# Eight expert jobs as one pipeline, with the rows returned through a DRAM scratch and the expert weights in contiguous blocks

## The chip, the cores and the metric

One core of a Trainium2 chip runs the whole program. The metric is the device time of one launch in microseconds; the kernel before has a median of 1696.33 us in 3 runs (1695.38 to 1701.48). The host's work on the inputs ahead of the launch is not in it.

## The reference

Two layers over 256 tokens of width 1024, all in float32:

```
h = h + swa_sink_attention(rms_norm(h), ...)      # layer 0
h = h + swiglu(rms_norm(h), f_gate, f_up, f_down)
h = h + gated_deltanet(rms_norm(h), ...)          # layer 1
h = h + moe(rms_norm(h))
out = rms_norm(h)

def moe(h):                                       # D_FF = 3584, 8 experts, top 2
    logits = h @ w_router;  top_w = softmax(top_k(logits, 2))
    for e in range(8):
        y = (silu(h @ w_gate[e]) * (h @ w_up[e])) @ w_down[e]
        out += combine[:, e:e+1] * y              # combine is 0 where e isn't chosen
```

Each expert has three matrices of 1024 x 3584, 44 MB in float32. On average 64 of the 256 tokens choose an expert.

## The kernel before

Four stages follow each other: attention, FFN, gated DeltaNet (GDN) and the experts. The change is in the last, which starts at about 633 us.

**Precision.** A float32 product is made of three matmuls in the type f32r (mm3, L282 to 285): high by high, high by low and low by high. So each weight block is split in two. `fetch` (L262) brings 1 MB from DRAM to one of six raw slots, `split_high` (L267, ScalarE) rounds it to w_high, `split_low` (L273, VectorE) takes the rest as w_low. The split pair has three slots. Counting semaphores tie these together: a fetch of block n waits until block n-6 has been split low, a high split of n until TensorE has used block n-3.

**A job.** The tokens of an expert are packed into 128 rows ("slots"). A job is one expert on its 128 slots; if an expert has over 128 tokens there is a second job for it, up to 11 in all. In this run there are 8, one for each expert; jobs 8 to 10 are skipped by a test on a value that the kernel computes (`njobs`). A job goes through 7 chunks of 512 columns of D_FF. A chunk uses six blocks: two of gate (0, 1), two of up (2, 3), two of down. For a chunk TensorE does 24 matmuls of gate into PSUM bank 0, 24 of up into bank 1, four transposes of the activation (`turned`, L1275), and 24 matmuls of down that add up in banks 2 and 3 over the job. The gate of the next chunk is issued ahead of `turned` of this one, so that silu (ScalarE) and the product m_act (VectorE) are behind matmuls. In steady state block numbers of a step are 4, 5 (gate of the next chunk), 6, 7 (its up), 8, 9 (down of this one), 10, 11 (gate of the one after), and ScalarE and VectorE take them in this order, with silu, m_act and m_act_high/low between.

**Between jobs.** The last chunk has no gate of a next one beside it. The kernel instead turns the next job's rows (`turn_in`, L1302, eight transposes of x_slots, which ScalarE and VectorE split to x_high and x_low), does `turned` and down, and then, in the next turn of the loop:

- ScalarE and VectorE copy the job's result from banks 2 and 3 as ys_high and ys_low;
- TensorE does gate of the first chunk, then `back(j)` (L1292): eight matmuls of pickT, a 0/1 matrix that puts the slots back to their tokens, into banks 4 to 7; then two matmuls that turn the next `pick` into bank 1, which VectorE copies to pickT, and only then up, which writes bank 1;
- VectorE adds banks 4 to 7, times the router's weight, to h (`add`, L1812), and makes the next `pick`.

The first `back` has no job before it: its operands are cleared to zero (L1805 to 1807). The last follows the loop, and after it the final norm.

**Rows in.** POOL scatters the normed tokens to a DRAM scratch of 12 x 128 rows by indirect DMAs (`fill_slots`), cleared in the FFN stage (`clear_slots`), and loads 128 rows for each job from 1 on. Job 0 gets its rows by a gather on TensorE (L1254 on).

**Reads of the weights.** SP reads w_gate and w_up as [128 partitions x 4 x 512] with rows of 2 KB and w_down as [128 x 2 x 1024] with rows of 4 KB, out of the matrices as they are given.

Of the kernel before, what the change touches and what calls it, by code (L numbers as in the profile page):

```python
# [12 lines left out]
D = 1024  # L13
T = 256
TT = T // 128
# [58 lines left out]
def hybrid_kernel(nc, x, a_norm, a_w_qkv, a_b_qkv, a_sinks, a_w_o, f_norm, f_w_gate, f_w_up, f_w_down,  # L74
                  b_norm, b_w_in, b_conv_w, b_a_log, b_dt_bias, b_o_norm, b_w_o,
                  m_norm, m_w_router, m_w_gate, m_w_up, m_w_down, final_norm, consts, out,
# [12 lines left out]
    with ExitStack() as ctx:  # L89
# [81 lines left out]
        with ExitStack() as c:  # L171
# [23 lines left out]
            xg = sb("x_slots", [128, D], c=c)  # L195
            late, row_e, row_s = (sb(n, R8, c=c) for n in ("late", "row_e", "row_s"))
# [4 lines left out]
        x_dram = nc.dram_tensor("x_slots_dram", ((JOBS + 1) * 128, D), f32, kind="Internal").ap()  # L201
        NJ = 15
# [91 lines left out]
        def _(sp):  # L294
# [45 lines left out]
            if "moe" in stages:  # L340
                def job(j, e):
                    ffn_stream(base["moe"], j * NC, m_w_gate[0, ds(e, 1)], m_w_up[0, ds(e, 1)], m_w_down[0, ds(e, 1)],
                               lambda i: j * NC + i)
# [17 lines left out]
        def _(pool):  # L361
# [18 lines left out]
            def clear_slots():  # L380
                link(nc.gpsimd.memset(zeros[:], 0.0))
                for j in range(JOBS + 1):
                    pool.dma_start(x_dram[128 * j:128 * j + 128, :], zeros[:]).then_inc(sem("slots_clear"), 16)

            def fill_slots():
# [12 lines left out]
                pool.dma_start(xg[:], x_dram[128:256, :]).then_inc(sem("xg_in"), 16)  # L398
                njobs = pool.value_load(jobs[0:1, NJ:NJ + 1], min_val=E, max_val=JOBS)
                with pool.Fori(1, JOBS) as j:  # L400
                    with pool.If(j < njobs):
                        pool.wait_ge(sem("gather_ps"), j + 1)
                        pool.dma_start(xg[:], x_dram[ds((j + 1) * 128, 128), :]).then_inc(sem("xg_in"), 16)
# [83 lines left out]
        def _(act):  # L487
# [111 lines left out]
            def deltanet(n0):  # L599
                act.wait_ge(sem("slots_clear"), 16 * (JOBS + 1))  # L600
                act.dma_start(o_w[:], bcast(b_o_norm[0])).then_inc(loaded_gdn, 16)
# [154 lines left out]
            def experts(n0):  # L756
# [9 lines left out]
                nc.scalar.activation(w1[:], gap[:], ACT.Exp).then_inc(sem("gap_exp"), 1)  # L766

# [14 lines left out]

                act.wait_ge(sem("jobs_done"), 1)
                njobs = act.value_load(jobs[0:1, NJ:NJ + 1], min_val=E, max_val=JOBS)
                with act.Fori(0, JOBS) as j:
                    with act.If(j < njobs):
                        def silu(n, r):
                            act.wait_ge(w_used, n + r * RAW)
                            nc.scalar.activation(mg[:], PS[:, 0, :], ACT.Silu).then_inc(sem("m_silu_done"), 1)

                        def turned(c):
                            act.wait_ge(sem("m_turn_ps"), j * NC + c + 1)
                            nc.scalar.activation(maH[:], PS[:, 4, :].rearrange("p (f q) -> p f q", f=4), ACT.Copy)\  # L793
                                .then_inc(sem("m_high_done"), 1)

                        r0 = j * NC
                        split_high(act, n0 + 2, r0)
                        split_high(act, n0 + 3, r0)
# [3 lines left out]
                        with act.Fori(0, NC - 1) as i:  # L802
                            r = j * NC + i
                            split_high(act, n0 + 6, r)
                            split_high(act, n0 + 7, r)
                            turned(i)
                            split_high(act, n0 + 8, r)
                            act.wait_ge(sem("m_act_done"), j * NC + i + 1)
                            silu(n0 + 6, r)
                            for n in range(9, 12):  # L810
                                split_high(act, n0 + n, r)
                        turned(NC - 1)
                        turned_in(j + 1)
                        with act.If(j + 1 < njobs):
                            split_high(act, n0 + SUBS_FFN, r0)
                            split_high(act, n0 + SUBS_FFN + 1, r0)
                        act.wait_ge(sem("back_ps"), j + 1)
                        act.wait_ge(w_used, n0 + SUBS_FFN + r0 * RAW)
                        nc.scalar.activation(ysH[:].rearrange("p (b n) -> p b n", b=2), PS[:, 2:4, :], ACT.Copy)\
                            .then_inc(sem("ys_high"), 1)  # L820
# [13 lines left out]
        def _(pe):  # L834
# [402 lines left out]
            def experts(n0):  # L1237
# [73 lines left out]
                with pe.Fori(0, JOBS) as j:  # L1311
                    with pe.If(j < njobs):
                        def gate(n, r):
                            gate_up(n, r, 0).then_inc(w_used, 1)

                        def up(n, r):
                            gate_up(n, r, 1).then_inc(w_used, 1)

                        r0 = j * NC
                        pe.wait_ge(sem("gather_low"), j + 1)  # L1320
                        gate(n0, r0)
                        back(j)
# [585 lines left out]
```

## Time and profile before

| | us |
|---|---|
| median of 3 runs | 1696.33 |
| span of the profiled execution | 1695.6 |
| TensorE busy (matmuls) | 1564.9 |
| VectorE busy | 1245.4 |
| ScalarE busy | 1017.5 |
| POOL busy | 79.7 |

The span runs from the first to the last instruction; the device time of the three runs is this and the little that lies around it, so the two stand 0.7 us apart at the median. The profiled execution moved 446.03 MB in 190790 DMA packets, 430.83 MB of them on SP's queue. Matmuls of 512 columns show as 0.39 us each but start every 0.23 us, as they are pipelined: starts tell more than durations. In the rows PEclk is the granted TensorE clock as a share of 2.4 GHz, and a DMA share over 1 means that packets of several queues or blocks overlapped on an engine. "[0.88 <-PE PS L285]" behind an instruction is the time that its engine stood idle ahead of it and what ended that.

### The profile page before, as it was taken

The page shows a single profiled execution, that of the slowest core. Times are in us where ns is not written, and L with a number is a line of the kernel's source. Part 1 is how long each engine was busy: PE and PEld are TensorE (multiplying, and loading weights), DVE is VectorE, ACT ScalarE, POOL GpSimd, SP SyncE. Part 2 cuts the span into 40 slices and gives each one's busy share as a digit, 9 for nine tenths or more (in the row PEclk, how much of TensorE's full clock was granted, in tenths as well). Part 3 has the DMA queues.
Part 4 walks back from the last instruction along what each step waited for, and adds up shares of the span by engine and source line. Part 5 has one row for each costly group of instructions (what it writes and reads, how often), then busy time and mean ns, then how long its engine had stood idle before and what let it go on. Part 6 is the DMA issues. An engine that isn't in the chain of part 4 may idle for free.

```text
span 1695.6 us, 22769 instructions
## 1 busy us (share of the span) xinstructions
PE 1564.9 (92%) x8311; PEld 1308.0 (77%) x8311; DVE 1245.4 (73%) x1044; ACT 1017.5 (60%) x949; POOL 79.7 (5%) x89
## 2 busy tenths in 40 slices
PE   5888999998987877999999999999999999999996
PEld 4777888878986866887887887887887887887885
DVE  4745555545674446888888888888888888888886
ACT  4444434334853334677677677677777777777774
POOL 0002000000223112000000000000000000000000
PEclk9789999999999796999999999999999999999999
DMA  9317655552430212999999999999999999999992
GB/s 329 98 39 275 220 174 194 176 174 100 133 117 28 75 62 97 347 361 351 344 368 349 336 387 337 345 372 344 341 369 351 336 374 349 341 372 339 361 368 88
DMA packets 190790, 446.03 MB, mean 263 GB/s; under 512 B 9632, under 2 KB 10016, under 8 KB 190752
## 3 DMA queue, kind: packets, MB, share of 16 engines
q1 hardware_dynamic: 184032, 430.83, 71.1%
q0 software_dynamic: 3456, 12.58, 1.9%
q10 hardware_dynamic: 3264, 2.08, 0.4%
q8 instruction: 27, 0.44, 0.1%
q14 instruction: 11, 0.09, 0.0%
HBM read 436.03 MB, written 9.44 MB: 263 GB/s over the span
## 4 chain that ended last, share of the span: by engine, by line
PE 84%; DVE 6%; ACT 5%; issue 3%; ACTq 1%; DVEq 1%; POOL 0%; POOLq 0%
PE PS L283 25%; PE PS L285 25%; PE PS L284 25%; DVE w_low L275 2%; ACT w_high L271 2%; PE PS L1277 1%; PE PS L846 1%; PE PS L920 1%; PE PS L1162 1%; ACT xs L520 1%; ACT L271 1%; PE PS L896 0%; PE PS L1153 0%; PE PS L1209 0%; PE PS L909 0%
## 5 line engine op out<-in xcount | busy, mean ns | idle before, releaser
L275 DVE TENSOR_TENSOR w_low<-w_raw,w_high 128x2048 fp32r<-128x2048 f32 x408 | 934.0, 2296 | 247.6 <-ACT w_high L271 247.4
L271 ACT ACTIVATE w_high<-w_raw 128x2048 fp32r<-128x2048 f32 x408 | 781.2, 1917 | 393.9 <-PE PS L285 393.0
L283 PE MATMUL PS<-w_high,x_high 128*128 128x512 f32 x1264 | 503.5, 398 | 23.7 <-DVE pickT L1838 15.1
L285 PE MATMUL PS<-w_high,x_low 128*128 128x512 f32 x1264 | 495.6, 392 | 0.0
L284 PE MATMUL PS<-w_low,x_high 128*128 128x512 f32 x1264 | 494.9, 392 | 0.0
L283 PEld LDWEIGHTS PS<-w_high,x_high 128*128 128x128 f32 x1264 | 239.5, 189 | 76.8 <-DVE w_low L275 22.4
L285 PEld LDWEIGHTS PS<-w_high,x_low 128*128 128x128 f32 x1264 | 238.8, 189 | 51.5
L284 PEld LDWEIGHTS PS<-w_low,x_high 128*128 128x128 f32 x1264 | 239.4, 189 | 48.4
L283 PE MATMUL PS<-w_high,m_act_high 128*128 128x512 f32 x448 | 177.9, 397 | 11.9 <-DVE m_act_low L1831 11.9
L285 PE MATMUL PS<-w_high,m_act_low 128*128 128x512 f32 x448 | 177.2, 395 | 0.0
L284 PE MATMUL PS<-w_low,m_act_high 128*128 128x512 f32 x448 | 177.1, 395 | 0.0
L283 PEld LDWEIGHTS PS<-w_high,m_act_high 128*128 128x128 f32 x448 | 84.2, 188 | 33.3 <-issue 13.8
L285 PEld LDWEIGHTS PS<-w_high,m_act_low 128*128 128x128 f32 x448 | 84.2, 188 | 20.4
L284 PEld LDWEIGHTS PS<-w_low,m_act_high 128*128 128x128 f32 x448 | 84.2, 188 | 19.7
L793 ACT ACTIVATE m_act_high<-PS 128x512 fp32r<-128x512 f32 x56 | 33.6, 599 | 82.3 <-PE PS L1277 82.3
L283 PE MATMUL PS<-x_high,w_high 128*128 128x256 f32 x192 | 57.0, 297 | 0.0
L284 PE MATMUL PS<-x_low,w_high 128*128 128x256 f32 x192 | 55.9, 291 | 0.0
L285 PE MATMUL PS<-x_high,w_low 128*128 128x256 f32 x192 | 55.7, 290 | 0.0
L846 PE MATMUL PS<-cst,xs 128*128 128x128 f32 x96 | 21.6, 417 | 32.6 <-DVE xs L1384 25.2
L1398 DVE TENSOR_TENSOR h<-PS,h 128x512 f32<-128x512 f32 x36 | 22.5, 684 | 32.9 <-PE PS L285 32.9
L283 PE MATMUL PS<-w_high,f_act_high 128*128 128x512 f32 x112 | 45.5, 406 | 1.0 <-DVE f_act_low L1526 1.0
L846 PEld LDWEIGHTS PS<-cst,xs 128*128 128x128 f32 x96 | 19.4, 223 | 34.5 <-DVE xs L1384 26.8
(271 smaller groups left out, 1364.9 us busy)
## 6 DMA issues: line engine op xcount, KB each, us to landing
w_raw<-in_m_w_gate SPq DMA_DIRECT2D x112, 1024.0 KB, 7.2
w_raw<-in_m_w_up SPq DMA_DIRECT2D x112, 1024.0 KB, 7.1
w_raw<-in_m_w_down SPq DMA_DIRECT2D x112, 1024.0 KB, 6.7
w_raw<-in_b_w_in SPq DMA_DIRECT2D x16, 1024.0 KB, 5.5
w_raw<-in_f_w_gate SPq DMA_DIRECT2D x14, 1024.0 KB, 5.1
w_raw<-in_f_w_up SPq DMA_DIRECT2D x14, 1024.0 KB, 5.1
w_raw<-in_f_w_down SPq DMA_DIRECT2D x14, 1024.0 KB, 4.9
w_raw<-in_a_w_qkv SPq DMA_DIRECT2D x6, 1024.0 KB, 13.9
```

Of the source, the lines that this page charges most:

```text
L271: nc.scalar.activation(WH[:, n % SPLIT, :], W[:, n % RAW, :], ACT.Copy).then_inc(hi_done, 1)
L275: nc.vector.tensor_tensor(WL[:, n % SPLIT, :], W[:, n % RAW, :], WH[:, n % SPLIT, :].bitcast(f32), ALU.subtract).then_inc(lo_done, 1)
L283: nc.tensor.matmul(o, sH, mH, start=first, stop=False)
L284: nc.tensor.matmul(o, sH, mL, start=False, stop=False)
L285: return nc.tensor.matmul(o, sL, mH, start=False, stop=last)
L520: nc.scalar.activation(xs[:, t], h[:, t], ACT.Square, accum_out=ss[:, n, t:t + 1]).then_inc(ss_done, 1)
L793: nc.scalar.activation(maH[:], PS[:, 4, :].rearrange("p (f q) -> p f q", f=4), ACT.Copy)\
L846: last = nc.tensor.transpose(PS[:, 4 + b, 256 * kk + 128 * t:256 * kk + 128 * t + 128], src[:, t, 128 * k:128 * k + 128], ident)
L920: last = nc.tensor.matmul(PS[:, 6 + a % 2, 64 * hh:64 * hh + 64], probT[:, a % 2, hh * (t + 1) + kt, :], qkv[:, kt, 1280 + 64 * g:1280 + 6 ...
L1162: last = nc.tensor.matmul(PS[halves(s), A + s, HALF * hh:HALF * hh + HALF], Zt[halves(s), t, hh, :], X[halves(s), t, hh, :], start=True, s ...
L1277: last = nc.tensor.transpose(PS[:, 4, 128 * f:128 * f + 128], ma[:, 128 * f:128 * f + 128], ident)
L1398: return V.tensor_tensor(h[:, t, cb * CH:(cb + 1) * CH], PS[:, bank, :], h[:, t, cb * CH:(cb + 1) * CH], ALU.add)
```

## The change

The loop over jobs 0 to 7 becomes one pipeline of 56 chunks. Every step is the same on each engine: gate of the next chunk, `turned`, up of the next chunk, down of this one, also where the next chunk belongs to the next job. In the step ahead of a job's last, TensorE turns the next job's rows behind up. In the first step of a job ScalarE copies banks 2 and 3 (the result of the job before) to `ys`, and POOL stores that to a second DRAM scratch, `y_slots`. So `back`, pickT and `add` are left out for jobs 0 to 6. After job 6's store POOL gathers, by four indirect DMAs, for every token the row of each of its two experts, and VectorE adds them to h with the weights w0 and w1 while the last down runs. Job 7 (`LAST`) still returns through pickT. Rows 7 x 128 and on of the scratch are cleared to zero in the FFN stage, so that tokens of job 7 and of jobs over 7 add nothing there. Jobs 8 to 10 run, if there are any, one after the other behind that.

The host writes the experts' weights as one array of 1 MB blocks in the order in which they are read, gate, up of a chunk and down of the one before; each block is [128 partitions x 2048] with 8 KB of a partition in one piece. SP reads them one after the other. Block 2 of the first job is now split ahead of the gather instead of behind it.

```
+        y_dram = nc.dram_tensor("y_slots_dram", ((JOBS + 1) * 128, D), f32, kind="Internal").ap()
+        LAST = E - 1
+        Y_CLEAR = JOBS + 1 - LAST
...
+                def fetch_block(n, r, m):
+                    if n >= RAW:
+                        sp.wait_ge(lo_done, n - RAW + 1 + r * RAW)
+                    sp.dma_start(W[:, n % RAW, :], m_w_blocks[m] if isinstance(m, int) else m_w_blocks[ds(m, 1)].rearrange("a p c -> p (a c)"))\
+                        .then_inc(w_in[n % RAW], 16)
+
...
-                with sp.Fori(0, E) as j:
-                    job(j, j)
+                for k in range(4):
+                    fetch_block(n0 + k, 0, k)
+                with sp.Fori(0, E * NC - 1) as q:
+                    for k in range(6):
+                        fetch_block(n0 + 4 + k, q, 6 * q + 6 + k)
+                for k in range(2):
+                    fetch_block(n0 + 4 + k, E * NC - 1, E * SUBS_FFN + 4 + k)
...
+                for j in range(LAST, JOBS + 1):
+                    pool.dma_start(y_dram[128 * j:128 * j + 128, :], zeros[:]).then_inc(sem("y_stored"), 16)
...
+                def store(j):
+                    pool.wait_ge(sem("ys_out"), j + 1)
+                    pool.dma_start(y_dram[ds(j * 128, 128), :], ys[:]).then_inc(sem("y_stored"), 16)
+
+                with pool.Fori(0, LAST - 1) as j:
+                    pool.wait_ge(sem("gather_ps"), j + 2)
+                    pool.dma_start(xg[:], x_dram[ds((j + 2) * 128, 128), :]).then_inc(sem("xg_in"), 16)
+                    store(j)
+                store(LAST - 1)
+                pool.wait_ge(sem("y_stored"), 16 * (Y_CLEAR + LAST))
+                for c in range(2):
+                    for t in range(TT):
+                        nc.gpsimd.indirect_dma_start(yg[:, c, t], None, y_dram[:, :], bass.IndirectOffsetOnAxis(ap=slot[:, c, t:t + 1], axis=0))\
+                            .then_inc(sem("yg_in"), 16)
...
+                split_high(act, n0 + 2)
...
+                def y_out(j):
+                    act.wait_ge(w_used, n0 + 4 + (j + 1) * NC * RAW)
+                    act.wait_ge(sem("y_stored"), 16 * Y_CLEAR + 16 * j)
+                    nc.scalar.activation(ys[:].rearrange("p (b n) -> p b n", b=2), PS[:, 2:4, :], ACT.Copy).then_inc(sem("ys_out"), 1)
+
...
+                def step(q, out_of=None, x_of=None):
+                    split_high(act, n0 + 6, q)
+                    if out_of is not None:
+                        y_out(out_of)
+                    split_high(act, n0 + 7, q)
+                    turned(q)
+                    split_high(act, n0 + 8, q)
+                    act.wait_ge(sem("m_act_done"), q + 1)
+                    silu(n0 + 6, q)
+                    split_high(act, n0 + 9, q)
+                    if x_of is not None:
+                        turned_in(x_of)
+                    split_high(act, n0 + 10, q)
+                    split_high(act, n0 + 11, q)
+
+                split_high(act, n0 + 3)
+                silu(n0 + 2, 0)
+                split_high(act, n0 + 4)
+                split_high(act, n0 + 5)
+                step(0)
+                with act.Fori(0, LAST) as j:
+                    with act.Fori(1, NC - 2) as i:
+                        step(j * NC + i)
+                    step(j * NC + NC - 2, x_of=j + 1)
+                    step(j * NC + NC - 1)
+                    step(j * NC + NC, out_of=j)
+                with act.Fori(LAST * NC + 1, E * NC - 1) as q:
+                    step(q)
+                turned(E * NC - 1)
+                y_high(n0 + 6, E * NC - 1)
...
+                def pick_turned(c):
+                    pe.wait_ge(sem("pick_done"), c + 1)
+                    for t in range(TT):
+                        last = nc.tensor.matmul(PS[:, 7, 128 * t:128 * t + 128], pick[:, t, :], identR[:], start=True, stop=True)
+                    last.then_inc(sem("pickT_ps"), 1)
+
...
+                def step(q, first=False, final=False, x_of=None, x_wait=None, out_of=None):
+                    pe.wait_ge(sem("m_silu_done"), q + 1)
+                    if x_wait is not None:
+                        pe.wait_ge(sem("gather_low"), x_wait + 1)
+                    gate(n0 + 4, q)
+                    pe.wait_ge(sem("m_act_done"), q + 1)
+                    turned()
+                    up(n0 + 6, q)
+                    if x_of is not None:
+                        turn_in(x_of)
+                    pe.wait_ge(sem("m_low_done"), q + 1)
+                    if out_of is not None:
+                        pe.wait_ge(sem("ys_out"), out_of + 1)
+                    down(n0 + 8, q, first, final)
+
                 gather(0)
+                pe.wait_ge(sem("gather_low"), 1)
+                gate(n0, 0)
+                pe.wait_ge(sem("slot_done"), 1)
+                up(n0 + 2, 0)
+                step(0, first=True)
+                with pe.Fori(0, LAST) as j:
+                    with pe.Fori(1, NC - 2) as i:
+                        step(j * NC + i)
+                    step(j * NC + NC - 2, x_of=j + 1)
+                    step(j * NC + NC - 1, final=True, x_wait=j + 1)
+                    step(j * NC + NC, first=True, out_of=j)
+                with pe.Fori(LAST * NC + 1, E * NC - 1) as q:
+                    step(q)
+                pick_turned(1)
+                pe.wait_ge(sem("m_act_done"), E * NC)
+                turned()
+                pe.wait_ge(sem("m_low_done"), E * NC)
+                down(n0 + 4, E * NC - 1, False, True)
+                back(0)
...
+                split_low(dve, n0 + 2)
                 gathered(0)
...
-                V.memset(ysH[:].bitcast(f32), 0.0)
-                V.memset(ysL[:].bitcast(f32), 0.0)
-                V.memset(pickT[:].bitcast(f32), 0.0).then_inc(sem("pickT_done"), 1)
-                dve.wait_ge(sem("pickT_done"), 1)
-                dve.sem_inc(sem("ys_low"), 1)
-                dve.sem_inc(sem("added"), 1)
...
+                def step(q, x_of=None):
+                    split_low(dve, n0 + 6, q)
+                    split_low(dve, n0 + 7, q)
+                    turned(q)
+                    split_low(dve, n0 + 8, q)
+                    split_low(dve, n0 + 9, q)
+                    gated(q + 1, n0 + 8, q)
+                    if x_of is not None:
+                        turned_in(x_of)
+                    split_low(dve, n0 + 10, q)
+                    split_low(dve, n0 + 11, q)
+
+                split_low(dve, n0 + 3)
+                split_low(dve, n0 + 4)
+                gated(0, n0 + 4, 0)
+                split_low(dve, n0 + 5)
+                step(0)
+                with dve.Fori(0, LAST) as j:
+                    with dve.Fori(1, NC - 2) as i:
+                        step(j * NC + i)
+                    step(j * NC + NC - 2, x_of=j + 1)
+                    step(j * NC + NC - 1)
+                    step(j * NC + NC)
+                picks(LAST, slice(0, 128))
+                with dve.Fori(LAST * NC + 1, E * NC - 1) as q:
+                    step(q)
+                turned(E * NC - 1)
+                pick_turned(0)
+                dve.wait_ge(sem("yg_in"), 16 * 2 * TT)
+                for c, weight in enumerate((w0, w1)):
+                    for t in range(TT):
+                        if c:
+                            dve.wait_ge(sem("added"), t + 1)
+                        V.scalar_tensor_tensor(out=h[:, t], in0=yg[:, c, t], scalar=weight[:, t:t + 1], in1=h[:, t],
+                                               op0=ALU.mult, op1=ALU.add).then_inc(sem("added"), 1)
+                dve.sem_inc(sem("added"), 4 * LAST)
+                y_low(0)
+                add(0, LAST)
...
+def expert_blocks(gate, up, down):
+
+    g = gate.reshape(E, 2, 4, 128, NC, CH).transpose(0, 4, 1, 3, 2, 5).reshape(E, NC, 2, 128, SUB)
+    u = up.reshape(E, 2, 4, 128, NC, CH).transpose(0, 4, 1, 3, 2, 5).reshape(E, NC, 2, 128, SUB)
+    d = down.reshape(E, NC, 2, 2, 128, D).transpose(0, 1, 2, 4, 3, 5).reshape(E, NC, 2, 128, SUB)
+    blocks = np.zeros((E * NC + 1, 6, 128, SUB), np.float32)
+    blocks[:E * NC, 0:2] = g.reshape(E * NC, 2, 128, SUB)
+    blocks[:E * NC, 2:4] = u.reshape(E * NC, 2, 128, SUB)
+    blocks[1:, 4:6] = d.reshape(E * NC, 2, 128, SUB)
+    return blocks.reshape(6 * (E * NC + 1), 128, SUB)
```

## Rows read from the trace of the kernel before

**Rows 1.** the page's first part, busy time of each engine

```profile
PE 1564.9 (92%) x8311; PEld 1308.0 (77%) x8311; DVE 1245.4 (73%) x1044; ACT 1017.5 (60%) x949; POOL 79.7 (5%) x89
```

**Rows 2.** stretches: us; PE, PEld, DVE, ACT, POOL busy; PEclk, DMA share, GB/s

```profile
20.00:24.00 4.00, 2.76 (x8) 1.94 (x7) 3.26 (x9) 3.15 (x9) 0.00 (x0) 1.00 1.04 393
801.50:928.00 126.50, 122.86 (x553) 100.35 (x552) 109.98 (x67) 91.52 (x62) 0.54 (x1) 1.00 0.97 354
837.00:854.00 17.00, 17.00 (x77) 13.92 (x77) 14.86 (x8) 12.41 (x9) 0.00 (x0) 1.00 1.03 380
```

**Rows 3.** the chain that ended last, in order of time, of 620 to 830

```profile
691.36 0.44 PE PS L1277 x4
...
776.23 0.44 PE PS L1277 x4
...
787.74 0.87 PE PS L1305 x8
788.62 0.45 PE PS L1277 x4
...
817.50 0.44 PE PS L1277 x4
```

**Rows 4.** TensorE's waits, 676 to 1690: us, times, longest

```profile
PE PS L283 <- DVE pickT L1838: 15.1, 8, 2.5
PE PS L283 <- DVE m_act_low L1831: 11.9, 8, 1.5
PE PS L283 <- DVE w_low L275: 2.8, 8, 0.4
```

**Rows 5.** TensorE in order of time, 663 to 680

```profile
664.97 0.79 PE L283 MATMUL PS<-w_high,x_high 128*128 128x512 f32 x1 [4.55 <-DVE x_low L1769]
...
673.34 0.39 PE L1298 MATMUL PS<-ys_high,pickT 128*128 128x512 f32 x1
...
677.98 0.79 PE L283 MATMUL PS<-w_high,x_high 128*128 128x512 f32 x1 [2.46 <-DVE pickT L1838]
```

**Rows 6.** all engines in order of time, a steady chunk

```profile
1098.36 1.92 ACT L271 ACTIVATE w_high<-w_raw 128x2048 fp32r<-128x2048 f32 x1 [0.88 <-PE PS L285]
...
1102.63 3.12 SPq L265 DMA_DIRECT2D w_raw<-in_m_w_up  x2
...
1109.53 0.40 PE L283 MATMUL PS<-w_high,m_act_high 128*128 128x512 f32 x1
...
1111.80 2.28 DVE L275 TENSOR_TENSOR w_low<-w_raw,w_high 128x2048 fp32r<-128x2048 f32 x1
...
1115.13 0.39 PE L283 MATMUL PS<-w_high,x_high 128*128 128x512 f32 x1
```

**Rows 7.** the blocks w_raw issued from 837 to 854

```profile
DMA to landing us min/median/max: 6.5/7.7/7.8
```

**Rows 8.** x_high and x_low in order of time, end of job 7

```profile
1672.69 1.08 ACT L780 ACTIVATE x_high<-PS 128x512 fp32r<-128x512 f32 x2
...
1673.80 1.29 DVE L1779 TENSOR_TENSOR x_low<-PS,x_high 128x512 fp32r<-128x512 f32 x2 [0.29 <-ACT x_high L780]
```

**Rows 9.** the chain that ended last, 1655 to 1696

```profile
1671.72 0.45 PE PS L1277 x4
...
1679.55 1.03 ACT ys_high L819
...
1680.60 1.24 DVE ys_low L1862
...
1691.27 1.28 DVE fin L1883
```

**Rows 10.** ScalarE in order of time, 655 to 690

```profile
660.46 2.17 ACT L771 ACTIVATE x_high<-PS,cols 128x128 fp32r<-128x128 f32 x8 [10.58 <-PE PS L1261]
...
670.49 1.92 ACT L271 ACTIVATE w_high<-w_raw 128x2048 fp32r<-128x2048 f32 x1 [4.63 <-PE PS L285]
```

**Rows 11.** line 789: ns min/median/max, first and last start

```profile
L789 ACT ACT_TABLE_LOAD  x8: 1283/1283/1283, 672.4 to 1559.5; - x8
```

More of the change, by code:

```diff
@@ L796, in experts @@
                         r0 = j * NC
[L797 to L798 removed]
+                        turned_in(j)
+                        for n in range(4):
+                            split_high(act, n0 + n, r0)
                         silu(n0 + 2, r0)
@@ L802, in experts @@
                         with act.Fori(0, NC - 1) as i:
[L803 to L820, printed above, removed]
+                            step(r0 + i)
+                        turned(r0 + NC - 1)
+                        y_high(n0 + SUBS_FFN, r0)
             if "att" in stages:
@@ L1321, in experts @@
                         gate(n0, r0)
-                        back(j)
-                        for t in range(TT):
-                            last = nc.tensor.matmul(PS[:, 1, 128 * t:128 * t + 128], pick[:, t, :], identR[:], start=True, stop=True)
-                        last.then_inc(sem("pickT_ps"), 1)
-                        pe.wait_ge(sem("pickT_done"), j + 2)
-                        up(n0 + 2, r0)
-                        def chunk(i, r, first):
-                            pe.wait_ge(sem("m_silu_done"), j * NC + i + 1)
-                            gate(n0 + 4, r)
-                            if first:
-                                pe.wait_ge(sem("added"), j * 4 + 5)
-                            pe.wait_ge(sem("m_act_done"), j * NC + i + 1)
-                            turned()
-                            up(n0 + 6, r)
-                            pe.wait_ge(sem("m_low_done"), j * NC + i + 1)
-                            down(n0 + 8, r, first, False)
@@ new lines, in pick_turned, with y_low @@
+                def pick_turned(c):
+                    dve.wait_ge(sem("pickT_ps"), c + 1)
+                    V.tensor_copy(pickT[:], PS[:, 7, 0:256].rearrange("p (t c) -> p t c", t=TT))
+                def y_low(c):
+                    dve.wait_ge(sem("ys_high"), c + 1)
+                    V.tensor_tensor(ysL[:].rearrange("p (b n) -> p b n", b=2), PS[:, 2:4, :],
+                                    ysH[:].bitcast(f32).rearrange("p (b n) -> p b n", b=2), ALU.subtract).then_inc(sem("ys_low"), 1)
@@ L1843, in experts @@
+                        r0 = j * NC
+                        e = dve.value_load(jobs[0:1, ds(j + 1, 1)], min_val=0, max_val=E - 1)
+                        picks(e, slice(128, 256))
+                        turned_in(j)
+                        pick_turned(j - LAST)
+                        for n in range(4):
+                            split_low(dve, n0 + n, r0)
                         split_low(dve, n0 + 4, r0)
-                        gated(0, n0 + 4, r0)
+                        gated(r0, n0 + 4, r0)
@@ L1864, in experts @@
-                final = dve.value_load(jobs[0:1, ds(njobs, 1)], min_val=0, max_val=E - 1)
-                add(njobs, final)
-                dve.wait_ge(sem("added"), njobs * 4 + 5)
+                            step(r0 + i)
+                        turned(r0 + NC - 1)
+                        y_low(j - LAST)
+                        add(j - LAST, e)
+                dve.wait_ge(sem("added"), njobs * 4 + 4)
                 dve.sem_inc(h_done, TT)
@@ L1897 @@
     arrays, args = {}, []
+    blocks = expert_blocks(*(np.asarray(inputs[name])[0] for name in ("m_w_gate", "m_w_up", "m_w_down")))
     for name in _INS:
-        a = np.ascontiguousarray(inputs[name])
+        a = blocks if name == "m_w_blocks" else np.ascontiguousarray(inputs[name])
         arrays[f"in_{name}"] = a
```

123 lines of the change are left out of this document (57 added, 66 removed).

## The prediction

> **What bounds the kernel now.** I read the page first. TensorE works for 1564.9 us of a span of 1695.6 us, 92%, and no other engine passes 73% [rows 1]. I then cut the span into stretches. From about 675 us on, everything is the experts' stage. It uses the granted clock at its full level, and within 126 us of a job TensorE works some 123 us, with the 16 DMA engines busy 0.97 of the time at 354 GB/s [rows 2]. So two resources are near their end there, and the question is which of them is hit first when the gaps go.
>
> The chain of work that ended last, in order of time, gives the rhythm. The four transposes of a chunk (L1277) come at 691.36 and at 776.23 five chunks later: 84.87/5 = 16.97 us a chunk [rows 3]. The last chunk of a job has no next gate matmuls but eight transposes of the next rows (0.87 us): 776.23 to 788.62 is 12.39 us. From there to the next job's first transposes, 817.50, it takes 28.88 us. A job is thus 84.87 + 12.39 + 28.88 = 126.14 us, while seven chunks at 16.97 would be 118.8. The 7.3 us between are the boundary, and the chain passes eight of these (the first without a job ahead of it).
>
> The waits of TensorE over the whole stage name what stands in a boundary: pickT 15.1 us in 8 times, m_act_low 11.9 in 8, w_low 2.8 in 8: together 3.7 us for one [rows 4]. Beside them are the eight matmuls of `back` and the two that turn `pick`; in job 0 they fill 673.34 to the start of a wait of 2.46 us that ends at 677.98, 2.2 us [rows 5].
>
> Inside a chunk TensorE waits for nobody. It is busy for 17.00 of 17.00 us, VectorE for 14.86 and ScalarE for 12.41 [rows 2]; ScalarE's splits stand idle for TensorE (0.88 us), not the reverse [rows 6], and blocks land in 7.7 us [rows 7].
>
> **The change, part by part.**
>
> *Boundaries between jobs, 7 of them.* `back`, the turn of `pick`, the wait for pickT and the additions to h go from jobs 0 to 6. The gate of the next job's first chunk fills the hole in the last chunk, so the wait for m_act_low goes too. What is left is a row of equal steps and the eight transposes. A job becomes 7 x 16.97 + 0.87 = 119.7 us in place of 126.1, 6.4 less. As a check: 2.2 us of matmuls and 3.7 of waits are 5.9; the rest I put down to the slower first matmul behind each of the three waits.
>
> Is something late in the new step? The transposes of rows move the end of up from 1109.5 to 1110.4 in the clock of rows 6. ScalarE then does x_high (1.08) to about 1111.7 and only then split 10 (1.92) to 1113.6. VectorE, which went from m_act to w_low 10 at 1111.80, does x_low (1.29) first, to some 1113.2, and ends w_low 10 at 1113.7 + 2.28 = 1116.0. TensorE wants it when down ends, 1115.13 + 0.87 = 1116.0 [rows 6, 8]. That is a draw: at best no loss; at worst the restarts and hand-offs cost 2 us in each. I take 0.3, as the w_low wait of before was 0.4 at most: +2.1 us for 7. Splits 11 and the next 6 and 7 come in 0.5 us or more ahead of need.
>
> The copy of y to `ys` (priced by ys_high, 1.03 us [rows 9]) sits on ScalarE between splits 6 and 7 of the next step. Split 7 waits until the first half of gate is through, 2.7 us into the step, and would start at 3.1. Its w_low would be there at 7.6 where up's second half wants it at 8.6. Hidden. Without that cover it costs 1.03 a job. TensorE's down waits for `ys` at 11.4 us into the step, long after.
>
> *Head.* So far the gate of job 0 starts at 664.97, `back` of a zero block at 673.34, and up only at 677.98 after 2.46 us of idling; behind that gap a matmul takes 0.79 us in place of 0.39, as at the stage's first matmul [rows 5]. Now up follows gate at 673.34. Its second half wants w_low of split 3 at 676.1; split 3 starts at 670.49 as before, ends at 672.4, low at 674.8 [rows 10]. 24 matmuls, by down's 5.60 us from 1109.53 to 1115.13 with a little off, take 5.5 us [rows 6]. Up ends at 678.8. Then a series: table load (1.28) and silu (0.6) to 674.3, split 4 to 676.2, split 5 to 678.1; low 4 to 678.5, m_act behind up to 679.6, low 5 to 681.9. The gate of chunk 1 wants that for its second half at 681.5 and so ends at 684.7, and the first transposes come at 684.7 in place of 691.36: 6.7 less. Split 2 is moved ahead of the gather: ScalarE idles 10.58 us there for the gather [rows 10], so 1.92 + 2.28 us hide (if not, about 2 us on the head).
>
> *Sum for the middle.* Before: 691.36 to 1671.72, 980.4 us [rows 3, 9]. After: 54 chunks x 16.974 = 916.6, 7 x 0.87 = 6.1, the last chunk 12.39 - 0.87 + 0.4 (the pick's turn) = 11.9: 934.6. Less 45.8.
>
> *Tail.* y_high, y_low, `back` and four additions stay. New is the sum of four gathered 128x1024 blocks, 4 x 1.28 by the `fin` row, after m_act_low and pickT. It starts about 2.2 us after the last transposes (1671.72 in before's clock) and is over at 1679.4; y_low starts at 1680.60 [rows 9]. Hidden by 1.2 us. The tests for jobs 8 to 10, which are all skipped, now stand behind the additions: 0 to 1.5 us, I take 0.5.
>
> *DMA.* The weights' bytes are the same, 42 blocks of 1.05 MB a job, but in 119.7 us in place of 126.1. With a load and a store of 0.52 MB each they ask for (44.0 + 1.05)/119.7 = 376 GB/s. In steady chunks before it was already 6.29 MB/16.97 = 371. A window of one chunk shows 380, and the start of the kernel, where the queue is full, 393, with pieces of 2 KB (w_down's 4 KB) [rows 2]. The slack: a block issued at 1102.63 is wanted by the split that follows the one of 1098.36 by a chunk, at 1115.33, 12.7 us later, and it lands in 7.7 [rows 6, 7]. So I charge nothing. The five more zero blocks cleared in the FFN stage are 2.6 MB, 7 us of the DMA engines at 354 GB/s; only POOL issues them and only the start of the GDN stage waits for them, far later: I take 0 of 0 to 7 us. The new gather of y starts a chunk into the last job and has over 90 us to land. Whether 8 KB pieces that lie end to end go faster no row shows; I bound their rate by 350 and 393 GB/s, and take no change. A faster load is worth nothing while nobody waits for it.
>
> Sum: 1695.6 - 6.7 - 45.8 + 2.1 + 0.5 = 1645.7. The median of the runs is 0.7 above the profile's span, so 1646 us. Own range 1640 (no new stall) to 1654 (over 1 us at each boundary).
>
> **Rivals.**
>
> A, *the DMA engines become the bound.* For it: busy 0.97 over a job, 1.03 in a steady chunk [rows 2]. Were 371 GB/s the ceiling, a job would take 45.1 MB/371 = 121.6 us, 1.9 more, x8: 1661. The sign of it would be ScalarE waiting for w_raw. Against: flat landings and 5 us of slack for each block.
>
> B, *the DMA bound with a worse rate.* One mechanism and one point: each job must stream 45.1 MB, and the gain is gone at 45.1/(119.7 + 6.2) = 358 GB/s. If blocks that lie end to end in DRAM stream at, say, 350, a job is 128.9 us and the kernel 1646 + 8 x 9.2 = 1720: slower. For it: a job averaged 354. Against: that average is what TensorE asked for, gaps included; a single chunk went at 380.
>
> The Trainium skill, "HBM Reference", section "Specifications (TRN2)", gives about 358 GB/s as a core's share. By that rule the whole gain would be lost and the time about 1696, no change. The same page, "Specifications", says a core streaming alone goes well above this share, to about 425. The trace agrees with the latter so far, with 380 and 393 GB/s [rows 2]. I give the rule 2 in 100.
>
> C, *the boundary costs more than I see.* The new x_low chain is a draw, and ScalarE loads its table twice a job (2 x 1.28 us; [rows 11] has one of the two), which I expect to go, since the steps of all jobs now follow each other without another function between them. If both loads stay and x_low's chain slips, each boundary costs 3 us: 1646 + 19 = 1665.
>
> D, *better than the sum:* without stalls and tail it is 1643; 0.1 us less in each of 56 chunks, for a cause that I don't see, would make it 1638 or under.
>
> **Chances.** Forecast 0.76; A 0.08; B 0.04; the rule's no change 0.02; C 0.07; D 0.03. A difference under 0.5% (8.5 us) can't be told from none. Faster is forecast, A, C and D: 0.94; same 0.02; slower 0.04. The range from 1638 to 1664 takes in the forecast's own and A; C's end and B lie outside.
>
> **What would show it.** L1277's rows 16.97 us apart without a break across jobs, 17.8 to 18.3 where the rows are turned in; TensorE's waits on pickT and m_act_low once each; `back` run once, 8 matmuls, in place of nine times; first transposes near 684.7; DMA near 376 GB/s over a job; ACT_TABLE_LOAD for the silu once. ScalarE idle for w_raw would prove A or B; a w_low wait over 1 us seven times, C. The forecast is wrong if the chunk itself is no longer 16.97, or if the last step's DVE work pushes y_low.

## The result

The changed kernel takes 1644.32 us (median of 4 runs, 1642.25 to 1646.81) beside 1697.85 us for the kernel before (4 runs): a ratio of 0.969, 95% interval 0.9676 to 0.9703. Forecast were 1646 us, with 1638 to 1664 as the range. Timed again beside other kernels it took 1645.31 us in 5 runs, again 0.969 (0.9673 to 0.9708).

The page of the changed kernel, its span and busy times, answers to [rows 1]:

```profile
span 1642.8 us, 22310 instructions
...
PE 1539.7 (94%) x8225; PEld 1290.6 (79%) x8225; DVE 1213.8 (74%) x983; ACT 994.1 (61%) x931; POOL 94.8 (6%) x104
```

TensorE works 25 us less and the span is 53 us shorter. The chain that ended last, in order of time, for the same stretch as [rows 3] (the transposes of a chunk are L1346 now, those of the next job's rows L1374):

```profile
750.96 0.44 PE PS L1346 x4
...
767.93 0.44 PE PS L1346 x4
773.84 0.87 PE PS L1374 x8
...
785.79 0.44 PE PS L1346 x4
...
802.79 0.44 PE PS L1346 x4
```

The reader is to see that the beat doesn't break at the end of a job: 16.97 us, then 17.86 where the eight transposes of 0.87 us are put in, then 17.00, where the kernel before had 12.39 and 28.88. TensorE's waits over the stage, as in [rows 4]:

```profile
PE PS L288 <- DVE x_low L1864: 4.5, 1, 4.5
PE PS L1367 <- DVE ys_low L1917: 2.4, 1, 2.4
PE PS L288 <- DVE m_act_low L1927: 1.5, 1, 1.5
PE PS L288 <- DVE w_low L280: 0.3, 1, 0.3
```

Each stands there once, at the head or at the tail, and pickT is gone. In order of time, TensorE alone, as in [rows 5], the starts of the first gate and of the first and last transposes:

```profile
663.00 0.79 PE L288 MATMUL PS<-w_high,x_high 128*128 128x512 f32 x1 [4.46 <-DVE x_low L1864]
...
680.01 0.50 PE L288 MATMUL PS<-w_high,x_high 128*128 128x512 f32 x1 [0.25 <-DVE w_low L280]
...
682.88 0.60 PE L1346 MATMUL PS<-cst,m_act 128*128 128x128 f32 x4
```

```profile
1617.51 0.62 PE L1346 MATMUL PS<-cst,m_act 128*128 128x128 f32 x4
```

In the two profiled executions the difference of 52.8 us in span falls into four parts. The kernel before has its first gate at 664.97, its first transposes at 691.20 and its last at 1671.56 in the same view. Up to the first gate it is thus 2.0 less. From there to the first transposes: 26.23 to 19.88, 6.4 less. From the first to the last transposes of the stage: 980.4 to 934.6, 45.7 less. The rest, to the end: 24.0 to 25.3, 1.3 more.

### The profile page after: what moved, and what is told of

It is laid out like the page before. It is cut to its first block, busy times and chain, and to the rows that moved or that the text cites. A ratio compares the mean times of both kernels' runs of the same rounds, so it can differ in the third digit from the quotient of the medians.

```text
span 1642.8 us, 22310 instructions
## 1 busy us (share of the span) xinstructions
PE 1539.7 (94%) x8225; PEld 1290.6 (79%) x8225; DVE 1213.8 (74%) x983; ACT 994.1 (61%) x931; POOL 94.8 (6%) x104
## 4 chain that ended last, share of the span: by engine, by line
PE 90%; ACT 4%; DVE 4%; issue 1%; ACTq 1%; POOL 0%; DVEq 0%; POOLq 0%
PE PS L288 27%; PE PS L290 27%; PE PS L289 27%; PE PS L1346 1%; ACT w_high L276 1%; DVE w_low L280 1%; PE PS L915 1%; PE PS L1231 1%; PE PS L989 1%; ACT xs L560 1%; PE PS L1222 0%; PE PS L1278 0%; PE PS L978 0%; PE PS L965 0%; ACT prob L593 0%
```

## The experiments

**The schedule without the blocks, and the blocks without the schedule.** The first kernel is the changed one with the reads of before; the second is the kernel before with the host's blocks.

```
-                    sp.dma_start(W[:, n % RAW, :], m_w_blocks[...])
+                    fetch(sp, n + k, r, "cols", wide(w, e)[:, 4 * half:4 * half + 4, cs])
+                    fetch(sp, n + half, r, "rows", wide(m_w_down, e)[:, f, :])
```

> The pipeline of the changed kernel with the weights read as the kernel before reads them, from the given matrices in pieces of 2 and 4 KB. Theory (the schedule makes the whole gain, the DMA engines have room in either layout): within 3 us of the changed kernel, ratio 0.969, chunks 16.97 us apart, blocks landing in under 9 us, ScalarE never waits for w_raw. Rival (the blocks make the room that the pipeline needs; 371 GB/s was the ceiling of the old pieces): 121.6 us a job in place of 119.7, about 1660 us, ratio 0.978, and ScalarE waits for w_raw.

> The kernel before with the host's 1 MB blocks and nothing else. Theory: no one waits for a block there, so 1.000 within 0.002 of the kernel before, though blocks land some tenths of a microsecond sooner. Rival (contiguous blocks are worth something by themselves): ratio 0.995 or less.

> The changed kernel itself, timed beside the others. Both theories: ratio to the kernel before 0.969, 1644 us. It is the yardstick for the other three.

Measured: the schedule alone 1646.10 us, 0.9694 (0.9678 to 0.971); both, beside it, 1645.31 and 0.969; the blocks alone 1697.93 us in 12 runs, 0.9999 (0.9987 to 1.001). The gain is the schedule's. Here is a stretch of the schedule with the old reads (us; PE, PEld, DVE, ACT, POOL busy; PEclk, DMA share, GB/s), and how long its blocks took to land there:

```profile
820.00:940.00 120.00, 120.00 (x543) 98.35 (x541) 105.44 (x59) 88.57 (x60) 1.08 (x2) 1.00 1.01 376
```

```profile
DMA to landing us min/median/max: 5.8/7.4/8.7
```

And the same two views of the changed kernel:

```profile
820.00:940.00 120.00, 120.00 (x544) 98.38 (x543) 105.48 (x59) 88.37 (x60) 1.08 (x2) 1.00 0.98 377
```

```profile
DMA to landing us min/median/max: 5.8/6.9/7.8
```

TensorE works 120.00 of 120.00 us in both, at 376 and 377 GB/s. The blocks lower the DMA share from 1.01 to 0.98 and the landing from 7.4 to 6.9 us (7.1 in a second execution), and nobody is waiting for either in this stretch. Nor does anyone in the kernel before: with the blocks its landing from 700 to 1600 us falls from 7.1 to 5.6 us and its time stays.

At one place the expectation for the old reads, that ScalarE never waits for w_raw, missed. It is where POOL gathers the returned rows beside the loads, from 1528 us on (`in_m_w_gate` is one of the weights in the old layout):

```profile
ACT w_high L276 <- DMA w_raw<-in_m_w_gate: 3.6, 2, 2.8
PE PS L288 <- DVE w_low L280: 0.8, 1, 0.8
```

A block issued at 1533.67 took 14.35 us to land there. In the changed kernel the longest landing is 11.8 us and no engine waits for w_raw. From the first to the last transposes it is 935.8 us with the old reads and 934.6 with the blocks. So the room in the old layout runs out once in 56 chunks, for about 1 us, which the times of the two don't tell apart.

**How much room the DMA engines have.** Both kernels leave out two of the three products of gate, up and down and most of each low part, so that the blocks' arrival sets the pace.

```
-                            last = mm3(PS[:, bank, :], xH[...], xL[...], wh[:, kk], wl[:, kk], k == 0, k == KD - 1)
+                            last = nc.tensor.matmul(PS[:, bank, :], xH[:, k, 0:128], wh[:, kk], start=k == 0, stop=k == KD - 1)
+            nc.vector.tensor_tensor(WL[:, n % SPLIT, 0:256], W[:, n % RAW, 0:256], ...)
```

> The changed kernel with two of the three products of gate, up and down left out and the low part of each weight block made for 256 of its 2048 columns, so that in the experts' stage TensorE needs some 6 us a chunk and ScalarE 12.7 (6 x 1.92 + 2 x 0.6). What is then left is the rate at which blocks come. Theory (the DMA engines have room): over 393 GB/s, the fullest window of the kernel before; at 420 a chunk of 6.29 MB takes 15.0 us. Rival A of the prediction (ceiling about 371 to 380): 16.6 us or more a chunk. If ScalarE binds: 12.7 us.

> The same with the old reads in pieces of 2 and 4 KB (the same work left out). Theory: these pieces cost more each, so the ceiling is lower than with blocks but still over the 377 GB/s that the pipeline asks for: about 393 GB/s, 16.0 us a chunk. Rival (layout makes no difference to the rate): the same chunk as with blocks within 1%. Other rival: under 377 GB/s, 16.7 us or more.

Measured: 1539.01 us with blocks (ratio 0.9072, 0.9054 to 0.909), 1595.67 with the old reads (0.9406, 0.9387 to 0.9425). The stretches with blocks, what ScalarE waited for, and with the old reads:

```profile
800.00:1000.00 200.00, 138.68 (x384) 85.31 (x384) 53.51 (x110) 167.10 (x113) 2.16 (x4) 0.74 1.01 422
...
1200.00:1400.00 200.00, 137.21 (x386) 84.03 (x384) 53.01 (x110) 166.48 (x112) 1.61 (x3) 0.75 1.01 422
```

```profile
ACT w_high L276 <- DMA w_raw<-in_m_w_blocks: 129.9, 197, 1.9
```

```profile
800.00:1000.00 200.00, 140.78 (x364) 87.40 (x364) 49.47 (x102) 154.91 (x104) 1.62 (x3) 0.66 1.04 395
```

Here ScalarE does wait for w_raw, and the rate stands still: 422 GB/s with pieces of 8 KB, 395 with pieces of 2 and 4 KB. That is the number the prediction lacked. The pipeline asks for 377, so the old reads leave 5% of room and the blocks 12%; 6.29 MB take 14.9 and 15.9 us of a chunk's 16.97. The layout makes a real difference to the rate, and to this kernel only the 1 us at the gather.

**What the return of the rows was worth by itself.** In the kernel before, `back`, the turn of pick, pickT's copy and wait and the additions are left out for jobs 0 to 6, and so is the empty `back` ahead of job 0: eight places, seven boundaries and the head. Only the last return stays.

```
                         gate(n0, r0)
-                        back(j)
-                        for t in range(TT): ...    # the turn of pick
-                        pe.wait_ge(sem("pickT_done"), j + 2)
+                        pe.wait_ge(sem("slot_done"), 1)
                         up(n0 + 2, r0)
```

> The kernel before with the return of jobs 0 to 6 left out: no back, no turn of pick, no wait for pickT, no additions but the last, whose result is not the reference's. The gate of a next job is still not in a job's last chunk. Theory: of the 4 us that the return costs a boundary (2.2 of matmuls, 1.8 of waiting), about 0.6 comes back as a wait for w_low, since ScalarE's copy, table load and splits stand in series: 3.5 us x 8 = 28 less, about 1669, ratio 0.9835; the other 15 to 20 us of the change need the filled last chunk. Rival (the return is the whole boundary): 1650, ratio 0.972.

Measured: 1674.87 us, 0.9874 (0.9858 to 0.9891), 21.8 less, not 28. The chain in order of time and TensorE's waits:

```profile
783.02 0.45 PE PS L1277 x4
```

```profile
906.57 0.45 PE PS L1277 x4
...
915.44 1.28 ACT L271
...
918.69 2.30 DVE w_low L275
```

```profile
PE PS L283 <- DVE w_low L275: 12.7, 16, 1.8
PE PS L283 <- DVE m_act_low L1825: 11.9, 8, 1.5
```

From a job's last transposes to the next one's it is 123.55 us, against 126.13 in the kernel before (788.62 to 914.75 in its chain). Only 2.6 us of the 4.0 taken away are saved at a boundary, 18.1 at seven; another 4.1 us are the head's. The wait for w_low has gone from 2.8 us in 8 times to 12.7 in 16: behind a job's last down ScalarE copies the result, loads its table and makes two splits, one after the other, and up's second half waits for the last of them. The wait for pickT had hidden that. A boundary lost 6.4 us in the changed kernel. The other 3.8 are put down to the next job's gate in the last chunk, which takes this series apart; that is the difference of two runs, and no run had the filled last chunk with the return still in place.

**TensorE's own work.** Ten matmuls are put back at each of the 7 boundaries, without waits.

```
                     gate(n0 + 4, q)
+                    if out_of is not None:
+                        for k in range(8):
+                            nc.tensor.matmul(PS[:, 7, :], xsH[:, 0, 0:128], xsH[:, 1, 0:CH], start=True, stop=True)
+                        # and two of 128 columns
```

> The changed kernel with the ten matmuls of a returned job put back at each of the 7 boundaries, behind the gate of the first step (eight of 512 columns, two of 128, on operands and a bank that nobody needs), but without their waits. Theory (TensorE sets the pace of every step, so its work counts in full): 2.2 us at each, 15 us more than the changed kernel, about 1660, ratio 0.978. Rival (a step has room that matmuls can fill, for instance behind a late w_low): under 10 us.

Measured: 1660.53 us, 0.9787 (0.9762 to 0.9812): 15 to 16 us more than the changed kernel. Its chain shows one of the seven, and the step around it:

```profile
787.96 0.44 PE PS L1346 x4
...
804.95 1.84 PE PS L1396 x8
806.97 0.46 PE PS L1346 x4
```

The step takes 19.01 us in place of 17.00, and the ten matmuls 2.01 of them (2.2 were expected). Seven times this is 14.1 us. The other 2.1 us by which the profiled execution is longer lie ahead of the experts' stage, which starts at 665.12 in place of 663.00. TensorE's work counts in full.

**The draw in the step that turns the rows in.** VectorE's x_low is made a second time there, into a tile nobody reads.

```
                     for b in range(2):
+                        V.tensor_tensor(ysL[...], PS[:, 5 + b, :]..., xH[...], ALU.subtract)
+                    for b in range(2):
```

> The changed kernel with VectorE's x_low of each next job computed a second time, into a tile that nobody reads, just ahead of the real one: 1.3 us more in the step in which the rows are turned in. Theory (the low part of the next gate block ends 0.2 us ahead of need there, as the trace of the changed kernel shows): a wait of 0.7 to 1.2 us at each of 7 boundaries, 5 to 8 us more than the changed kernel. Rival (there is more slack than that reading says): 1 us or less in all.

Measured: 1648.47 us, 0.9714 (0.9698 to 0.973). The chain and the wait:

```profile
770.88 0.45 PE PS L1346 x4
...
789.35 0.44 PE PS L1346 x4
```

```profile
PE PS L288 <- DVE w_low L280: 2.7, 8, 0.3
```

The step is 18.47 us in place of 17.86: 0.6 at each boundary, 4.3 in all (the medians differ by 3 to 4), with a wait of 0.3 and a slower first matmul. Adding 1.3 us of work cost 0.6, so VectorE's slack comes to about 0.7 us. Two gaps in the changed kernel's trace, shown below, make it up: w_low 10 is there 0.2 us ahead of need, and VectorE stands idle 0.45 us before it, until ScalarE has split block 10. In that step ScalarE's series of x_high and split 10 is what w_low waits for, not x_low. The size is under what was expected (5 to 8), the direction is the theory's.

**The head.** Block 2 is split behind the gather again.

```
-                split_high(act, n0 + 2)          # ahead of gathered(0)
+                split_high(act, n0 + 2)          # behind it, and so on VectorE
```

> The changed kernel with block 2 of the first job split where it was before, behind the gather. Theory (ScalarE and VectorE idle for the gather, and the early split takes a whole split out of the series that follows): up of the first chunk waits for w_low, some 2 us on the head and no more; ratio 0.970. Rival (the head's gain of 6.4 us comes from this move): 4 to 6 us, ratio 0.972.

Measured: 1648.81 us, 0.9719 (0.9694 to 0.9744; runs from 1646.37 to 1652.33). TensorE in order of time:

```profile
665.49 0.80 PE L288 MATMUL PS<-w_high,x_high 128*128 128x512 f32 x1 [4.46 <-DVE x_low L1864]
...
682.52 0.50 PE L288 MATMUL PS<-w_high,x_high 128*128 128x512 f32 x1 [0.27 <-DVE w_low L280]
...
685.38 0.60 PE L1346 MATMUL PS<-cst,m_act 128*128 128x128 f32 x4
```

From the first gate to the first transposes it is 19.89 us, as in the changed kernel (19.88). The move is worth nothing there, where 2 us were expected. What the head gained has two parts. `back`, the turn of pick and the wait for pickT lie between gate and up in the kernel before (673.34 to 677.98, 4.6 us). Behind that wait the granted clock is at half, the level of 1.2 GHz, and the first eight matmuls of up take 3.4 us for 1.8. The kernel before there, and the changed one in its up:

```profile
678.00:681.00 3.00, 3.00 (x7) 2.42 (x8) 3.00 (x7) 0.00 (x0) 0.00 (x0) 0.50 1.01 414
```

```profile
671.50:676.50 5.00, 5.00 (x24) 4.14 (x23) 3.66 (x2) 4.62 (x4) 0.61 (x1) 1.00 0.86 297
```

In the kernel before without the return the same stretch takes 22.09 us. There VectorE still clears ys_high, ys_low and pickT (2.1 us) and reads a value ahead of the low part of block 2, and up waits for it:

```profile
673.91 0.50 PE L283 MATMUL PS<-w_high,x_high 128*128 128x512 f32 x1 [1.82 <-DVE w_low L275]
```

The changed kernel has no such clears, which the prediction didn't name; in the kernel before they were over at 671.3, ahead of `back` at 673.34.

The whole stage stands 2.5 us later in the profiled execution than in the changed kernel's, and from the first transposes on it is the same within 0.2 us. The four runs are 3.5 to 4.5 us longer at the median than the changed kernel's nine; their two longest have a mean granted clock of 0.956 and 0.957, the other two 0.960. In the profiled execution the stage itself is the same, so there it isn't the move; what made the other runs longer was not settled, and the interval reaches to 0.9694.

**The tail, bank by bank.** The last down does bank 2 first and then bank 3, and the copy, the low part and the return of each follow on their own. A second kernel also puts the three tests for jobs 8 to 10 on VectorE behind one.

```
+                for b in range(2):
+                    for f in range(4): ... mm3(PS[:, 2 + b, :], maH[:, f, :], maL[:, f, :], ...)
+                    last.then_inc(w_used, 1)
+                for b in range(2):
+                    pe.wait_ge(sem("ys_low"), b + 1) ...
```
```
+                with dve.If(njobs > E):
                     with dve.Fori(E, JOBS) as j:
```

> The changed kernel with the last down, the copy of its result and the return of job 7 done bank by bank: bank 2's matmuls first, its copies beside bank 3's matmuls. Theory: the chain behind the last matmul of down was copy 1.03, low part 1.24, eight matmuls 1.9 to 3.5, four additions 2.8 us; half of each leaves the chain, about 4 us less than the changed kernel (1640, ratio 0.9665). Rival (VectorE's four additions of gathered rows, 4.9 us beside the down, push the first low part back): 1 us or less.

> The tail bank by bank, and VectorE's three tests for jobs 8 to 10 behind one test of whether there is any. In the run bank by bank the tests stood open behind the additions for about 1.2 us, of which this takes some 0.8. Theory: span from the end of the last down to the final norm's first square 4.5 us, where the changed kernel has 8.7 and the tail bank by bank 5.3; time 3 to 4 us under the changed kernel, ratio 0.967. Rival (these are hidden or lost in the spread): no difference from 0.969.

Measured: 1643.25 us, 0.9673 (0.9657 to 0.969), and 1641.69, 0.9668 (0.965 to 0.9687). The chain of the second, then of the changed kernel:

```profile
1627.56 0.61 ACT ys_high L875
...
1631.67 1.06 ACT xs L560
```

```profile
1625.55 1.03 ACT ys_high L841
...
1626.60 1.24 DVE ys_low L1917
...
1627.88 0.50 PE PS L1367
...
1630.94 0.44 PE PS L1368
...
1631.41 0.56 DVE h L1907
...
1634.22 1.06 ACT xs L560
```

From the end of down to the final norm's first square: 4.1 us (1627.54 to 1631.67) in place of 8.7 (1625.52 to 1634.22). With the banks alone it was 5.3, 3.4 us less than in the changed kernel, where about 4 were expected. The second version's five runs (1640.07 to 1642.15) all lie under the changed kernel's nine (1642.25 to 1648.80), but they were not timed side by side and the intervals of the ratios overlap, so the traces carry this and not the times.

## Why the prediction was right

*The sum.* The mechanism was the one forecast. That the number is only 1.7 us off is in part luck: the terms' errors are 2.1 us for stalls that did not come and 2.0 us ahead of the stage, both too long, against 0.3 at the head and 0.8 in the tail, both too short. The span was forecast as 1645.7 us and is 1642.8. The 0.7 us from span to time was off too: in every run on record with both, the time stands 1.5 to 1.8 us over the span (1644.39 and 1642.8 here).

*The boundaries.* 6.4 us less at each of 7, and 934.6 us from first to last transposes: the same to a tenth as forecast before the 2.1 us for new stalls. Those did not come. The changed kernel in order of time, around a step that turns rows in:

```profile
774.75 1.09 ACT L822 ACTIVATE x_high<-PS 128x512 fp32r<-128x512 f32 x2 [1.65 <-PE PS L1374]
```

```profile
775.94 1.28 DVE L1875 TENSOR_TENSOR x_low<-PS,x_high 128x512 fp32r<-128x512 f32 x2
...
777.67 6.93 DVE L280 TENSOR_TENSOR w_low<-w_raw,w_high 128x2048 fp32r<-128x2048 f32 x3 [0.45 <-ACT w_high L276]
```

The low part of block 10 starts at 777.67 and is there at 779.96; down ends and gate starts at 780.16. The forecast called this a draw and charged 0.3 us; it is won by 0.2. The charge was the mis-sized term, 2.1 us where the seven steps of 17.86 stand 0.1 over 16.97 + 0.87: the run with x_low twice shows how near it was.

*The head.* Forecast 6.7 less from the first gate to the first transposes, measured 6.4. The steps named (up right behind gate, a wait of 0.4 in chunk 1's gate, measured 0.25) are in the trace. The prediction saw one slow matmul behind the wait for pickT; it was eight, 1.6 us in all. Its sum held nonetheless, since it counted up's 24 matmuls at full pace (5.5 us, measured 5.45 from 671.42 to 676.87). That the early split of block 2 hides was right, but left at its old place it is hidden too: without the split ahead of the gather nothing is lost, where the prediction gave about 2 us.

*The tail.* Forecast 0.5 more, measured 1.3. The part named, the tests for skipped jobs, cost nothing here, since they ran beside VectorE's additions; they show only where these are shortened. What was not named are `back`'s matmuls: 0.43 us apart in the changed kernel (1627.88 to 1630.94 from the first to the last of eight), where in the kernel before they were 0.23 apart behind the same wait of 2.4 us. That is 1.4 us. The granted clock over these eight, in the changed kernel and in the kernel before:

```profile
1628.00:1631.40 3.40, 3.37 (x8) 2.11 (x8) 0.00 (x0) 0.00 (x0) 0.00 (x0) 0.54 0.02 5
```

```profile
1682.00:1684.00 2.00, 1.99 (x8) 1.30 (x8) 0.00 (x0) 0.30 (x1) 0.00 (x0) 1.00 0.00 0
```

The change isn't what sets this: with the old reads the pipeline has the same tail, and there they were 0.23 apart. The sum of the gathered rows was done in 4.86 us, from 1619.84, before y_low wanted VectorE at 1626.60: hidden, as forecast.

*Not in the sum: where the stage begins.* 2.0 us of the 52.8 came from ahead of the experts' stage. They are the rest of two differences. The stretch of attention and the GDN stage, of the kernel before and of the changed one:

```profile
50.00:130.00 80.00, 69.58 (x360) 58.03 (x359) 44.60 (x100) 35.84 (x97) 0.00 (x0) 0.79 0.20 64
380.00:640.00 260.00, 218.68 (x2254) 204.61 (x2253) 139.65 (x198) 126.04 (x243) 54.26 (x46) 0.92 0.27 88
```

```profile
50.00:130.00 80.00, 67.00 (x362) 55.23 (x360) 44.85 (x100) 36.99 (x100) 0.01 (x1) 0.85 0.21 66
380.00:640.00 260.00, 218.41 (x2248) 205.52 (x2246) 141.59 (x202) 126.09 (x245) 55.73 (x47) 0.89 0.25 86
```

TensorE first loads the FFN's activations at 186.1 and 181.2 us, 4.9 less, where attention had a granted clock of 0.79 and 0.85 of 2.4 GHz. From its last such load to the first gate of the experts it is 280.3 and 283.3 us, 3.0 more, at 0.92 and 0.89. Neither follows the kernel. The pipeline with the old reads has that first load at 186.2, the kernel before without the return at 181.8. The second stretch took 280.1 to 280.3 us in five executions, one of the kernel before and four with the pipeline, all at 0.92, and 283.2 to 283.3 in five, one of them of the kernel before without the return, at 0.89 and 0.90. The kernel before with the blocks took 288.5 at 0.89, so the clock is not all of it. The first gate thus stands between 663.0 and 670.8 us in the executions that were profiled. How much of the spread of the runs this makes was not measured.

The five more zero blocks cost nothing, as charged: from POOL's first value of the FFN's norm to its first of the GDN stage's it is 254.0 us in the kernel before (134.48 to 388.44) and 253.4 in the changed one (129.99 to 383.42).

*DMA.* The demand of 376 GB/s was right (377). Rival A put the ceiling at 371 and rival B at under 358; it is 395 with the old pieces and 422 with the blocks, so both were wrong for either layout. The share of 0.97 to 1.03 in the profile had looked like a resource at its end, but it reads 0.97 to 1.01 at 377 GB/s and 1.01 at 422: it does not tell the room that is left. Of the Trainium skill's "HBM Reference", "Specifications (TRN2)", 358 GB/s did not bind this core; what the same page says of a core that streams alone (about 425) agrees with the 422 measured. No run here had a second core at work.

*Rival C.* The table loads of each job went, as expected: two in each of 8 jobs before, one in the whole stage now. There was a part of it in the kernel before, though: the serial chain of copy, table load and splits, hidden behind the wait for pickT. The prediction added waits and matmuls of a boundary (3.7 + 2.2) as if each could be had by itself. For the whole change the sum is right, because the chain is taken apart too; for the return alone, even with 0.6 us taken off for w_low, it promised over a quarter too much (28 us expected, 21.8 measured).

## What to carry to other kernels

In a loop that TensorE fills, write down the steady step and multiply it; what a boundary costs is the rest. Here 2.6 of its 6.4 us went with the boundary's own work and waits, and all of it only when the next round's first work also stood in the last step of this one. A named wait is worth its length only if no other chain ends just behind it: take it away in a kernel by itself before counting on it. Whether a DMA share near 1 is a limit is seen from landing times that grow and from an engine that waits for a block; measure the ceiling by making the consumers cheap, as here, before a layout is changed for its sake.

## What the runs showed of the hardware

- Blocks of 1 MB read at 422 GB/s in pieces of 8 KB a partition, end to end, and at 395 in pieces of 2 and 4 KB. Landing took 12.3 and 13.5 us in place of about 7; by rate times landing some 5.2 and 5.3 MB were on their way, about five of the six slots.
- Behind equal gaps of 2.4 us in the tail, eight matmuls ran 0.23 us apart in four executions (one of the kernel before, one each with the blocks alone, with the old reads and with x_low twice), and 0.39 to 0.43 apart in three (twice the changed kernel, and with the late split). In two the pace changed among the eight: from 0.23 to 0.43 in the kernel before without the return, from 0.43 to 0.25 with the ten matmuls. What the granted clock does behind such a gap is not the same each time, and it isn't the change that decides.
